# Softmax attention with 32 units in four passes: the value products cut into three pieces inside the next pass, a third buffer for the turned probabilities, and the two output copies moved from the pass's start to its middle

## The reference, cut to what matters

```python
def _dense_attention(q, k, v):
    s = jnp.einsum('bqkgd,bskd->bkgqs', q, k).astype(jnp.float32) * ATT_SCALE
    p = jax.nn.softmax(s, axis=-1).astype(v.dtype)
    return jnp.einsum('bkgqs,bskd->bqkgd', p, v)
```

## Time and profile before

| what | value |
|---|---|
| median of 3 runs | 2618.85 us (2614.33 to 2620.21) |
| the profiled execution, its own time | 2625.77 us |
| span in the profile (first to last instruction) | 2624.0 us |
| PE busy | 2494.5 us, 95% of the span |
| the attention stage | about 2080 to 2188 us of the span, some 4% |

### The profile page before, as it was taken

The page is one execution under the profiler, slowest core; times in us unless marked ns, Lnnn a source line. Parts: engine busy times, 40 slices in busy tenths (PEclk is TensorE's granted clock), DMA queues, the critical chain, the costliest instruction groups (busy, mean ns, idle before and its releaser), DMA issues.

```text
span 2624.0 us, 38652 instructions
## 1 busy us (share of the span) xinstructions
PE 2494.5 (95%) x15967; PEld 2197.2 (84%) x15967; DVE 1384.1 (53%) x1896; ACT 838.5 (32%) x1208; POOL 265.8 (10%) x203
## 2 busy tenths in 40 slices
PE   6999999999999999999999999998997799899998
PEld 6999999998999999999987888886884456688886
DVE  6777656655554344542655666677117463533433
ACT  4423444434322122321314222223223363322321
POOL 2000222223100000200111000002003111000001
PEclk9999999989999999999778999999997899899998
DMA  3222533325222222222002544551320001122221
GB/s 133 81 74 77 125 83 87 87 57 203 81 89 89 97 80 96 98 81 81 33 1 85 185 147 160 176 176 64 120 80 16 0 1 48 61 89 101 89 94 64
DMA packets 93871, 235.47 MB, mean 90 GB/s; under 512 B 60074, under 2 KB 61700, under 8 KB 69556
## 3 DMA queue, kind: packets, MB, share of 16 engines
q1 hardware_dynamic: 88208, 201.40, 23.8%
q10 hardware_dynamic: 5540, 32.30, 3.5%
HBM read 222.00 MB, written 11.67 MB: 89 GB/s over the span
## 4 chain that ended last, share of the span: by engine, by line
PE 86%; DVE 9%; ACT 3%; issue 2%; DMA 1%; ACTq 0%; POOL 0%; DVEq 0%; POOLq 0%; SPq 0%
PE ps L298 67%; PE ps L1086 1%; PE ps L1076 1%; PE ps L1100 1%; PE ps L302 1%; PE ps L2492 1%; PE ps L2509 1%; DVE c_DA L1986 1%; PE ps L1878 1%; PE ps L462 1%; PE ps L1879 1%; PE ps L1113 1%; PE ps L1112 1%; DVE n_y L443 1%; PE ps L2500 1%
## 5 line engine op out<-in xcount | busy, mean ns | idle before, releaser
L298 PE MATMUL ps<-xa_hi,whi 128*128 128x264 f32 (+1 forms) x2512 | 654.0, 319 | 46.5 <-DVE wlo L321 20.7
L298 PE MATMUL ps<-xa_lo,whi 128*128 128x264 f32 (+1 forms) x2512 | 648.3, 317 | 0.0
L298 PE MATMUL ps<-xa_hi,wlo 128*128 128x264 f32 (+1 forms) x2512 | 646.8, 317 | 0.0
L321 DVE TENSOR_TENSOR wlo<-raw,whi 128x2048 fp32r<-128x2048 f32 x161 | 370.1, 2299 | 255.9 <-ACT whi L314 253.3
L298 PEld LDWEIGHTS ps<-xa_hi,whi 128*128 128x128 f32 x2512 | 416.7, 190 | 89.9 <-DVE wlo L321 22.9
L314 ACT ACTIVATE whi<-raw 128x2048 fp32r<-128x2048 f32 x161 | 307.5, 1910 | 572.7 <-PE ps L298 560.8
L298 PEld LDWEIGHTS ps<-xa_lo,whi 128*128 128x128 f32 x2512 | 416.0, 190 | 29.6
L298 PEld LDWEIGHTS ps<-xa_hi,wlo 128*128 128x128 f32 x2512 | 415.7, 190 | 30.0
L298 PE MATMUL ps<-xb_lo,whi 128*128 128x264 f32 (+1 forms) x1280 | 384.5, 341 | 0.0
L298 PE MATMUL ps<-xb_hi,whi 128*128 128x264 f32 (+1 forms) x1280 | 382.6, 339 | 1.5 <-DVEq L243 1.5
L298 PE MATMUL ps<-xb_hi,wlo 128*128 128x264 f32 (+1 forms) x1280 | 382.8, 340 | 0.0
(11 more groups left out here) (416 smaller groups left out, 2837.2 us busy)
## 6 DMA issues: line engine op xcount, KB each, us to landing
raw<-weights SPq DMA_DIRECT2D x161, 1024.0 KB, 4.8
mod_w<-weights_mod ACTq DMA_DIRECT2D x24, 1024.0 KB, 4.8
g_EC<-scr_g SPq DMA_DIRECT2D x10, 424.0 KB, 5.3
scr_z<-z_st SPq DMA_DIRECT2D x16, 264.0 KB, 4.7
g_D<-scr_g SPq DMA_DIRECT2D x10, 371.0 KB, 4.9
scr_a<-g_AT SPq DMA_DIRECT2D x10, 318.0 KB
h<-x_in ACTq DMA_DIRECT2D x4, 528.0 KB, 8.7
z_b<-scr_z SPq DMA_DIRECT2D x1, 2112.0 KB
```

The source lines that it names most:

```text
L298: mm = pe.matmul(ps[:, at_ + step * c + bank, 0:tn], w[:, hb.slot, k, c * P:(c + 1) * P], x[:, k, t0:t0 + tn], start=(k == 0 and n == 0), ...
L321: dve.tensor_tensor(wlo[:, hb.slot], raw[:, hb.raw_slot], whi[:, hb.slot].bitcast(F32), ALU.subtract).then_inc(S("w_lo"), 1)
```

## The change

The value products of a pass no longer run in one block at its end. They run in three pieces of two key tiles (four matmuls) each, behind the transposes of the first three units of the next pass. The values of the last pass keep their place behind everything. Since the next pass's first head would now overwrite `a_pT[0]` while the pieces still read it, a third buffer `a_pT2` takes the first head of every second pass. `high` moves on ACT from the copy of the pass's first unit to that of its fifth. `low` moves on DVE from the end of step n % 8 == 1 to that of step n % 8 == 5. The wait of ACT's copies for the values is kept only where it is needed.

```diff
+        a_pT2 = aa_r.take("a_pT2", [P, KEYS // P, SEQ])
...
+        def probs(it, y):
+
+            return a_pT2 if y == 0 and it % 2 else a_pT[y]
...
-            def values(it):
-                pe.wait_ge(S("at_q"), it * 3 + 3)
-                pe.wait_ge(S("at_lo"), it + 1)
-                pe.wait_ge(S("at_pT"), it * 8 + 9)
-                for t in range(KEYS // P):
+            def values(it, tiles):
+                if tiles[0] == 0:
+                    pe.wait_ge(S("at_q"), it * 3 + 3)
+                    pe.wait_ge(S("at_lo"), it + 1)
+                    pe.wait_ge(S("at_pT"), it * 8 + 9)
+                for t in tiles:
                     for y in range(2):
-                        mm = pe.matmul(ps[64 * y:64 * y + 64, 6, :], a_vst[:, t, :], a_pT[y][:, t, :], start=(t == 0),
+                        mm = pe.matmul(ps[64 * y:64 * y + 64, 6, :], a_vst[:, t, :], probs(it, y)[:, t, :], start=(t == 0),
                                        stop=(t == KEYS // P - 1))
-                mm.then_inc(S("at_o"), 2)
+                if tiles[-1] == KEYS // P - 1:
+                    mm.then_inc(S("at_o"), 2)
...
-                if n % 8 == 7:
-                    values(n // 8)
+                if n >= 8 and n % 8 < 3:
+                    values(n // 8 - 1, (2 * (n % 8), 2 * (n % 8) + 1))
+            values(N_IT - 1, range(KEYS // P))
...
-                if n % 8 == 0 and it:
+                if n % 8 == 4 and it:
                     high(it - 1)
                 act.wait_ge(S("at_T"), n + 3)
-                if b == 0:
-                    act.wait_ge(S("at_o"), it * 2 + (y + 1))
-                act.activation(a_pT[y][:, :, b * P:(b + 1) * P].rearrange("p (n a) t -> p n a t", n=2),
+                if b == 0 and it:
+                    act.wait_ge(S("at_o"), it * 2 + 2 * y)
+                act.activation(probs(it, y)[:, :, b * P:(b + 1) * P].rearrange("p (n a) t -> p n a t", n=2),
...
-                if n % 8 == 1 and it:
+                if n % 8 == 5 and it:
                     low(it - 1)
```

## The result

Over 20 runs of each kernel the changed one took 2626.57 us in the median (2615.99 to 2630.91), the one before 2616.30 us (2609.44 to 2630.80). The ratio is 1.0027, with a 95% interval of 1.0016 to 1.0038. So the change made the kernel slower by 0.27%, some 7 us (4.2 to 9.9). The two medians alone lie 10.27 us apart and the means 7.49; single runs of one kernel spread over 15 to 21 us, so I go by the ratio. The direction was the one of the forecast and the time lies in its range, but the size was nearer three times the +2.5 us of the sum, and beyond the 0.2% that I had given as "no change".

What follows compares the result with a forecast made beforehand. TensorE, busy for 95% of the span, was taken to bound the kernel. Three boundaries gave 3 x (1.76 - 0.93) = +2.5 us, on the median of 2618.85 us a forecast of 2621.35 (+0.10%), range 2614.5 to 2628.

Steps and rivals of the forecast that it cites:

- no change: Whole kernel: a time within 0.2% (5.2 us) of the one before; chance 0.77.
- What bounds the stage: The touched stage: PE all but full in ordinary units of 2.00 to 2.13 us, with nothing overlapping the next stage.
- The pieces and switches: Boundary between passes: 14.24 us with three pieces where it was 15.17, so 0.93 us less for each.
- The switch: Each piece's entry to and exit from half-array weights on PE: 0.37 us together, bounded by 0.25 and 0.74.
- The moved copies: `high` and `low` in full-speed units: the retention's step and sixth unit's transposes come 1.76 us later at each boundary.
- The third buffer and the waits: ACT's copy into the new buffer and GpSimd's copy of the values' weights: claimed to cost nothing.
- The sum: Three boundaries together: 3 x (1.76 - 0.93) = +2.5 us, or +0.10%.
- The clock: Rival, slower: the new stall puts one pass at 1.2 GHz, some 20 us more, 2641 us; chance 0.02.
- the dear switches: Rival, slower: each of nine pieces costs 0.99 us for switching in place of 0.37, +8.1 us, 2627.0; chance 0.14.
- slower: Whole kernel: slower by more than 0.2%; chance 0.05 + 0.12 + 0.02 = 0.19.
- the one without the stall: Rival, faster: `high` is through in time and only the boundary's saving counts, -2.8 us, 2616.1; chance 0.12.

Runs made afterwards that it cites:

- e4: Changed kernel with the values in one block behind the next pass's first unit's transposes and `low` at n % 8 == 7; ratio 0.9983 to the kernel before.
- e2: Kernel before with only `high` moved to n % 8 == 4 and `low` to n % 8 == 5, values still one block; ratio 1.0011 to the kernel before.
- e1: Changed kernel with `low` at the end of step n % 8 == 7 in place of 5; ratio 0.9982 to the kernel before.
- e5: Changed kernel again without an edit, profiled and timed a second time; ratio 1.0014 to the kernel before.
- e9: Changed kernel with three extra unread matmuls in the last pass's stall alone, ahead of unit 29's transposes; ratio 0.9996 to the kernel before.
- e10: Changed kernel with three extra unread matmuls in each stall of units 13 and 21, unit 29's left idle; ratio 1.0021 to the kernel before.
- e7: e4 with two extra unread matmuls ahead of each of the last two units' transposes and ahead of the last values; ratio 0.9988 to the kernel before.
- e8: Kernel before with extra unread matmuls ahead of the last two units' transposes and the last values; ratio 0.9989 to the kernel before.
- e12: Kernel before again without an edit, profiled and timed a second time; ratio 1.0000.
- e6: Changed kernel with the retention's step on VectorE at n % 8 == 7 in place of 6; ratio 1.0014 to the kernel before.

## Why the prediction was off in size

*What bounds the stage* was right: PE is full in ordinary units, and the time between the passes went as worked out. The next stage starts at the same distance behind `low` in every profile.

*The pieces and switches*: forecast 0.93 us less for a boundary, measured 0.97. The switch, sized at 0.37 us, is 4.06 - 3.71 = 0.35 in a pass's first piece and 4.01 - 3.71 = 0.30 in the others. That is 0.16 us less for a boundary, of which the unit ahead of the pieces takes back 0.11 (T7 to T8 2.11 us, where the sum had 2.00). From the other side, e4 has 0.49 for two switches, some 0.25 each. Of what a boundary won, 0.34 us came with the moved copies alone (e2), as the wait of 0.36 us went. The rule of the Trainium skill's page "TensorEngine Tiling (Array Packing)", section "Key Properties", that a change of the tiling mode drains the engine, agrees with these rows of 0.30 and 0.35 us.

*The moved copies*: forecast 1.76 us of stall for a pass, measured 1.70 or 1.71, and 1.76 in e2. DVE waited 0.99 us for `high`, where the prediction had about 1.2. The chain was the one named: copy, exponentials, `high`, `low`, retention's step, maximum, scaling, transposes. Moving `low` alone away from it (e1) removed all of it.

*The third buffer and the waits* cost nothing, as forecast: GpSimd's copy (L2485) ran at 2116.58, right behind the third piece, and the next first piece came at 2132.59.

*The sum* of these was +2.5 us and measured +2.2. That part of the forecast was right, and it left no more than no change.

*The step that failed is the rival "The clock"*. It said that the one idle stretch of 0.99 us did nothing to the clock, "so this is remote", and gave it 0.02, with a price of 20 us for a whole pass at 1.2 GHz. That the new idle time can let the clock fall was right, but both its chance and its price were wrong. The fall doesn't last a pass, it costs 0.75 to 3.7 us. And it is no rare case: it was there in every profile with the stall at unit 29, where I had looked at each idle stretch by itself. The trace of the kernel before had the rows for a better guess: three stretches of 0.99 us stand close together at the stage's end (the rows of before above), and the third new stall ends 0.9 us ahead of the first of them. In the changed kernel's two profiles the clock took 5.16 and 3.67 us, more than the orders' own 2.2. Together they are 7.4 and 5.9 us from T0. Both lie in the interval of the timed 7 us (4.2 to 9.9), and the orders' 2.2 alone don't. The second timing (e5, -1.0 to 8.4 us) allows all of them.

*Luck had a part in the range.* The measured 2626.57 us lies above the forecast's 2621.35 and below 2628 only because the dear switches had stretched the range to there, and they didn't come. By the prediction's own bar of 0.2% the outcome was "slower", which it had given 0.19, of which 0.02 was for the clock.

*The other rivals*: the one without the stall didn't come, for the reason given against it, as ACT reached `high` 2.44 us behind the fourth unit's transposes. Dear switches didn't come either.

*What stays open*: how often the clock falls in executions without the third stall. One profile a kernel (two of before and of the changed one) can't say, and the timings have intervals of 0.11% and more to either side. What decides whether a given idle stretch is followed by a fall stays open too, since one program differed between two profiles. And that the third stall rather than the others is what matters isn't shown: the profiles' count and the timings of e9 and e10 point to it, but the profiles of these two are alike and their intervals overlap.

## What to carry to other kernels

When work is moved out of an idle time into full-speed units, price the place it goes to first. The two copies had cost at most 0.34 us a pass behind the values (e2). In full-speed units they cost 1.7, because DVE's came late behind ACT's; with DVE's two steps later that stall was gone (4.51 us in place of 6.19). And where TensorE gets a new idle stretch, look for other idle stretches near it, since it may be several together that let the clock fall, which these runs suggest and don't show. Of these versions the ones with the values in the next pass and `low` at its end (e1, e4, e7) are the fastest, by 0.12 to 0.18%, and only e4's interval lies wholly below 1.

## What the runs showed of the hardware that I had not expected

The granted clock fell from 2.4 to 1.2 GHz behind 1.9 us of idle time of TensorE that followed long busy work, in one of ten cases in mid-stage, and it fell even behind two or three idle stretches of 0.99 us each with short work of 0.85 us between them (e4, e9), in two of six profiles. The same program showed the fall in mid-stage in one profile and not in another. Filling the stretches at the end with matmuls that nobody reads delayed nothing in e7 and e8, and the clock stayed at 2.4 GHz there. It did so in three of the four profiles with these stretches idle and no stall in any pass as well (before, e1, e12, but not e4), so that the filling keeps it there isn't shown. VectorE's scaling of 128x768 took 0.92 and 0.91 us in place of 0.62 the two times that it ran beside GpSimd's L2483 (e6).
